# GpSimd's first loads behind a wait, and another order of the middle projection's products

## The reference, cut to what matters

```python
h  = concat(meta_tokens, x)                    # 272 rows
xn = rms_norm(h, norm_mix_g)
proj = xn @ w_in                               # q, k, v of branch A | forget, cq, ckv, k_rope, k_idx, idx_w | gates
o_a = fox_attention(...)                       # branch A, 8 heads
cq_n = rms_norm(cq); c_kv = rms_norm(ckv)      # branch B: latent attention over 64 selected keys
o_b = dsa_attention(...)
h  = h + (sigmoid(ga) * (o_a @ w_branch_a) + sigmoid(gb) * (o_b @ w_branch_b)) @ w_out
h  = h + moe_ffn(rms_norm(h))                  # top 4 of 32 experts
out = rms_norm(h)[:, 16:]
```

## Time and profile before

| | |
|---|---|
| median of 3 runs | 1213.9 us |
| lowest, highest | 1212.64, 1214.19 us |
| span of the profiled execution (first to last instruction) | 1211.7 us |
| own time of that execution | not listed apart from the three runs; its span lies 0.9 to 2.5 us under them |
| mean granted TensorE clock | 0.984 of full speed |
| busy: PE, DVE, ACT, POOL | 93%, 24%, 18%, 1% |
| DMA | 433.55 MB, mean 358 GB/s |

### The profile page before, as it was taken

One profiled execution on the slowest core, in us unless ns is written; L12 is line 12 of the kernel. 1 busy time (PEld: TensorE's weight loads), 2 busy tenths in 40 slices (PEclk: granted clock), 3 DMA queues, 4 the chain that ended last, 5 costly groups with the idle time before them and its releaser, 6 DMA issues.

```text
span 1211.7 us, 14339 instructions
## 1 busy us (share of the span) xinstructions
PE 1131.7 (93%) x5508; PEld 527.8 (44%) x5508; DVE 292.5 (24%) x726; ACT 215.0 (18%) x354; POOL 14.3 (1%) x27
## 2 busy tenths in 40 slices
PE   6999999999999999999999999989899989899986
PEld 4877788664343433343434233323333333333332
DVE  2237443241121212212212121212121212121213
ACT  1436773031011000100111011001100110011001
POOL 3010000000000000000000000000000000000000
PEclk8999999999999999999999999999999999999999
DMA  9823225849999999999999999999999999999995
GB/s 280 249 70 105 91 84 197 334 163 412 419 415 420 416 419 416 419 416 419 416 419 416 419 416 419 416 419 417 418 417 418 418 418 418 417 418 417 418 418 215
DMA packets 93306, 433.55 MB, mean 358 GB/s; under 512 B 7726, under 2 KB 24272, under 8 KB 60480
## 3 DMA queue, kind: packets, MB, share of 16 engines
q1 hardware_dynamic: 92048, 429.99, 88.2%
q0 software_dynamic: 960, 2.30, 0.8%
q10 hardware_dynamic: 272, 0.93, 0.3%
HBM read 432.13 MB, written 1.05 MB: 358 GB/s over the span
## 4 chain that ended last, share of the span: by engine, by line
PE 46%; SPq 43%; DMA 4%; DVE 4%; issue 3%; ACT 0%; DVEq 0%
SPq L438 20%; SPq L442 17%; PE psum L1535 14%; PE psum L1565 9%; SPq L449 5%; PE psum L1376 4%; PE psum L1178 2%; PE psum L1356 2%; PE psum L1394 2%; DMA arena<-in_w_gate_up 2%; PE psum L1576 2%; DMA ring<-in_w_in 2%; PE psum L1425 1%; PE psum L1340 1%; PE psum L1512 1%
## 5 line engine op out<-in xcount | busy, mean ns | idle before, releaser
L1535 PE MATMUL psum<-arena 128*64 128x512 f32 x1024 | 232.7, 598 | 12.6 <-DMA arena<-in_w_gate_up 12.6
L1535 PE MATMUL psum<-ring,arena 128*64 128x512 f32 x1024 | 232.6, 598 | 11.6 <-DMA ring<-in_w_gate_up 11.6
L1054 DVE TENSOR_TENSOR arena<-psum,biasT 128x512 f32<-128x512 f32 x64 | 44.0, 688 | 439.9 <-PE psum L1512 439.9
L1535 PEld LDWEIGHTS psum<-arena 128*64 128x64 f32 x1024 | 68.4, 137 | 162.9 <-issue 123.8
L1535 PEld LDWEIGHTS psum<-ring,arena 128*64 128x64 f32 x1024 | 68.4, 136 | 162.2 <-issue 125.1
L1565 PE MATMUL psum<-ring,arena 128*64 128x512 f32 x512 | 119.5, 623 | 17.3 <-DVE arena L1065 17.3
L1565 PE MATMUL psum<-arena 128*64 128x512 f32 x512 | 115.0, 608 | 17.3 <-DVE arena L1065 17.3
L937 DVE TENSOR_TENSOR h<-h,psum 128x1024 f32<-128x1024 f32 x32 | 39.1, 1222 | 256.6 <-PE psum L1576 256.6
L679 ACT ACTIVATE arena<-psum 128x1024 f32<-128x1024 f32 x32 | 32.8, 1025 | 351.4 <-PE psum L1535 351.4
L1565 PEld LDWEIGHTS psum<-ring,arena 128*64 128x64 f32 x512 | 39.3, 143 | 91.9 <-issue 90.4
L1565 PEld LDWEIGHTS psum<-arena 128*64 128x64 f32 x512 | 38.7, 140 | 88.0 <-issue 87.8
(11 more groups left out here) (222 smaller groups left out, 786.3 us busy)
## 6 DMA issues: line engine op xcount, KB each, us to landing
arena<-in_w_gate_up SPq DMA_DIRECT2D x128, 1024.0 KB, 22.4
ring<-in_w_gate_up SPq DMA_DIRECT2D x128, 1024.0 KB, 21.9
arena<-in_w_down SPq DMA_DIRECT2D x48, 1024.0 KB, 22.4
ring<-in_w_down SPq DMA_DIRECT2D x48, 1024.0 KB, 21.8
arena<-in_w_down SPq DMA_DIRECT2D x32, 512.0 KB, 15.8
ring<-in_w_down SPq DMA_DIRECT2D x32, 512.0 KB, 16.1
ring<-in_w_in SPq DMA_DIRECT2D x14, 1024.0 KB, 8.6
ring<-in_w_out SPq DMA_DIRECT2D x4, 1024.0 KB, 5.0
```

Of the source, the lines that this page charges most:

```text
L1054: return v.tensor_tensor(dst.rearrange("p (m j) -> p m j", m=8), src, bias[:, m:m + 8, bass.ds(pair + e, 1)].broadcast_to([P, 8, CAP]), AL ...
L1535: ins = mm(bank[2 + 2 * e + n][h * CAP:(h + 1) * CAP, :], xg[:, c, e * CAP:(e + 1) * CAP], eslot(base + k)[:, h * D + n * 512:h * D + (n + ...
```

## The change

GpSimd issues the two norm vectors as before, then waits until slot 1 has landed, and only then issues the other ten loads; `w_uv` moves behind `w_uq` and `w_qidx` among them. On TensorE the block (1, 0) comes before (0, 1): both row tiles are multiplied by weight block 0 first, then both by weight block 1, and the meta tile's transposes move from between (1, 0) and (1, 1) to ahead of (0, 1). Nothing is computed otherwise.

```diff
             vector_rows(pool, q_norm_g, LATENT, 2, s_vec2)
             vector_rows(pool, kv_norm_g, LATENT + V_KV - V_Q, 1, s_vec2)
+
+            pool.wait_ge(slot_loaded[1], 16)
             for dst, src in ((bfor, b_forget), (klng, kln_g), (klnb, kln_b), (brt, b_router)):
                 pool.dma_start(dst[:], src.broadcast_to([P, dst.shape[1]])).then_inc(s_late, 16)
             pool.dma_start(kst[:, P:KCOLS], consts[:, P:KCOLS]).then_inc(s_kst, 16)
             pool.dma_start(wuk.rearrange("p (k r) -> p k r", k=4),
                            w_uk[0].rearrange("(k a) n r -> (a n) k r", a=2)).then_inc(s_mixw, 16)
+            pool.dma_start(wq[:, :, 0:768], w_uq[0].rearrange("(c p) n -> p c n", p=P)).then_inc(s_mixw, 16)
+            pool.dma_start(wq[:, :, 768:1024], w_qidx[0].rearrange("(c p) n -> p c n", p=P)).then_inc(s_mixw, 16)
             pool.dma_start(wuv.rearrange("p (h v) -> p h v", h=HEADS),
                            w_uv[0].rearrange("h r v -> r h v")).then_inc(s_mixw, 16)
-            pool.dma_start(wq[:, :, 0:768], w_uq[0].rearrange("(c p) n -> p c n", p=P)).then_inc(s_mixw, 16)
-            pool.dma_start(wq[:, :, 768:1024], w_qidx[0].rearrange("(c p) n -> p c n", p=P)).then_inc(s_mixw, 16)
...
             input_rows(0)
             mid_block(0, 0)
             input_rows(1)
-            mid_block(0, 1)
             mid_block(1, 0)
             input_rows(2)
+            mid_block(0, 1)
             mid_block(1, 1)
```

## The result

The changed kernel takes **1203.6 us** (median of 4 runs, 1203.17 to 1203.83) against 1214.05 for the kernel before, taken beside it (4 runs): a ratio of 0.9913, 95% interval 0.9899 to 0.9927. The forecast was 1205.0 us. The profiled execution's span is 1201.4 us instead of 1211.7.

A forecast was written before the change was run, and what follows sets the result against it. The start was taken as bound by transfers until 24.2 us, then by matmuls. Strips 10.4 us earlier less 1.7 for the clock gave 8.7, 1203.0 for the span, 1205.2 for the median, stated as 1205.0; range 1202.6 to 1209.0.

The forecast's parts named there:

- One for one to the end: Start to end of kernel: each us gained at the start counts fully at the end, 8.7 us in all.
- Landings: SP queue's early loads: slot 0 at 7.4 to 8.9, tile 1 at 8.9 to 9.7, slot 1 at 11.9 to 14.8.
- the early end: SP queue's early loads: q1 alone at 0.348 MB/us lands slot 0 at 7.4, tile 1 at 8.9, slot 1 at 11.9.
- the full-clock timeline's 26.2: TensorE's start: without half-clock stretches the strips start at 26.2 in place of 36.62, 10.4 us earlier.
- one half-clock stretch, 1.7 us: TensorE's start: one 3.4 us stretch at 1.2 GHz, costing 1.7 us of the 10.4; this case had 40%.
- the hole of today whose fall came at 10.2: TensorE, kernel before: wait for slot 0 from 8.5 to 13.2; clock at half 10.2 to 17.0, reason for charging 1.7 us.
- the full-clock case: TensorE's start: no half-clock stretch, 10.4 us gained, 1203.5 us; a quarter of all chance.
- The wait's price: Before slot 1 lands: GpSimd's loads on q0 take 9.4 us of all 16 engines, which the wait removes.
- The second rival: Early loads: q0 costs only its bytes, slot 0 at 11.6, gain 6.7 us with one half-clock stretch, 1207.2 us; chance 8%.
- The first rival: Start: only the new order counts, the wait removes nothing; 4.5 us gained, 1209.4 us; chance 4%.
- The order with the wait: TensorE's start: slot 1 is wanted at 19.2 instead of 15.1 and may come 4.4 us later than the late end.
- The cover of the late loads: GpSimd's small vectors at L757: `brt` at 24.8, wanted 29.5; cover 4.7 + 4.2 = 8.9 us; slower has chance 2%.

The follow-up runs named there:

- The wait alone: The changed kernel with the old order of the products, (0, 1) before (1, 0), GpSimd's wait kept: 1203.64 us, ratio 0.9916.
- wait_slot0_new: The changed kernel with GpSimd waiting for slot 0 in place of slot 1, new order of products kept: 1204.19 us, ratio 0.9916.
- wuv_as_before: The changed kernel with the load of w_uv back ahead of w_uq and w_qidx: 1203.58 us, ratio 0.9915.
- wait_slot7: The changed kernel with GpSimd waiting for slot 7 in place of slot 1: 1211.85 us, ratio 0.9984.
- wait_slot5: The changed kernel with GpSimd waiting for slot 5 in place of slot 1: 1205.27 us, ratio 0.9928.
- order_alone: The kernel before with only the new order of the products, GpSimd's loads as before: 1208.88 us, ratio 0.9955.
- big_first: The changed kernel with constants, weights and router (2.2 MB) in front of GpSimd's wait, the four small vectors behind it: 1212.67 us, ratio 0.9983.
- small_first: The changed kernel with the four small broadcast vectors (84 KB) back in front of GpSimd's wait: 1207.81 us, ratio 0.9952.

## Why the prediction was right, and where it was off

**What bounds the start** was read rightly: two transfers until 24.2, matmuls after it. The wait alone, and the two runs that put a part of the loads back in front of it, show that GpSimd's loads were the cause.

**One for one to the end** held: 1175.2 us from the strips on against 1175.1, in a spread of 3 us over the other profiles.

**Landings.** Slot 1 was put at 13.3 between 11.9 and 14.8; GpSimd's release at 13.86 agrees, and the four further profiles that show it have 13.77 to 14.59. The bounds for the other two failed. Tile 1 was put at 8.9 to 9.7 and came at 10.5. Slot 0 was put at 7.4 to 8.9, before tile 0's features. In the changed kernel's two profiles it was there for them, but in the other six profiles with a wait in front of all ten loads and no products of zeros TensorE waited for it, until 9.42 to 9.96. The step that failed is the early end: it lets a load land when the queue has moved its own sum of bytes. The queue had moved 2.44 MB when slot 0 (1.60) released GpSimd at 9.97 in `wait_slot0_new`, and 3.85 when slot 1 (3.19) did in the changed kernel. The prediction used such a lag, 0.87 MB, for slot 3 only. What the lag is made of was not tried.

Against that, tile 0's features were ready at 8.94 instead of 9.48, which I hadn't foreseen. 0.35 us of it is VectorE's scaling of tile 0, which took 0.75 us instead of 1.10. It took 1.05 to 1.23 in the four profiles in which GpSimd was issuing weight loads at that moment, and 0.75 in the other ten. The early features and tile 1's rows, 0.5 us late for TensorE, cancel, and so the full-clock timeline's 26.2 stood at 26.16. That is luck in part: in the three other profiles with a wait, the new order and full clock (`wuv_as_before`, `wait_slot7`, `wait_slot0_new`), where slot 0 came later, the strips started at 26.74 to 27.06.

**The clock is the term that was mis-sized.** I charged one half-clock stretch, 1.7 us, "because the hole of today whose fall came at 10.2 had begun like the first of these". The changed kernel had none in either profile. It isn't that none can come: of the eight profiles with the wait on a slot, all ten loads behind it and no products of zeros, two showed one over block (0, 0). The block then took 5.25 - 3.56 = 1.7 us longer, as I had it, but the strips moved by only some 1.0, because TensorE otherwise waits 0.4 to 0.7 us for tile 1's rows behind it. So the chance was too high and the price too: the full-clock case, 1203.5, had a quarter, and 1203.6 was measured. The changed kernel's two holes, 1.1 us and 2.6 us of which 1.1 are transposes, left the granted clock at 1.00. The length of the hole alone doesn't decide it: block (0, 0) ran at half clock after 1.31 us of waiting in `wait_slot5` and at full clock after 2.42 us in `order_alone`. What the Trainium skill says of transposes (TensorE: Matmul & The Clock Gate, "Part 4: PE-mode transpose") would have made two stretches the likelier end; for holes this short no run here shows two.

**The wait's price.** The 9.4 us of q0's engine time are 2.7 for the small vectors and 6.7 for the large loads, each measured apart. Taken off today's landing they gave slot 1 well (14.8 at the latest), slot 0 and tile 1 by 0.5 to 1.1 us too early. The second rival, bytes alone, is refuted by the result's slot 0 (there by 9.04, not at 11.6) and by the small vectors, which cost 4.2 us for 84 KB. The first rival, only the order, is refuted by the wait alone. Its price of 4.5 us for the order was about right (5.4 by the medians, though the profile accounts for 2.7 of them in the strips).

**The order with the wait.** I wrote that together with the wait it gives slot 1 slack. It does, but the slack isn't needed: slot 1 came before tile 1's transposes had ended. I hadn't worked out the old order with the wait, and it would have shown that (0, 1) covers tile 1's features, 1 us that the new order leaves as a hole. Where slot 1 does come late, at 20 in `big_first`, the new order's cover is real.

**The cover of the late loads** was right in place: the 4.2 us of slack behind L757 held in the run with slot 5 (3.3 us used), and ran out in the one with slot 7 (6.1 us lost of 10.8). Ahead of L757 there was more than the 4.7 us that I counted, since `brt` landed 6.0 us after its issue in the changed kernel, not 9.8.

## What to carry to other kernels

Before a kernel's first matmuls, look at which queue holds the DMA engines, in engine time and not in bytes, and hold back the loads whose first user comes late. Count how late that user is: here a wait for slot 1 or slot 0 was free, and one for slot 7 gave nearly all of the gain back. Work out both orders of the work again once the loads are in place, because an order that filled a hole can open another. A half-clock stretch that one execution shows is a chance and not a fixed price, so look at several profiles before you count it.

## What was unexpected of the hardware

- The same four broadcast loads (0.09 MB) held the 16 engines for 2.7 us in 6 to 11 us of `small_first` and for 0.4 us in 17 to 20.4 us of the changed kernel. Early they ran beside rows of x and 984-byte rows, late beside 1 KB rows alone. Which of this makes the difference was not tried.
- The landing of the first loads varies between executions in which the loads are the same: slot 0 released block (0, 0) at 13.20 in the kernel before and at 10.95 in `order_alone`, whose loads and whose work until then are the same.
- With the wait in place a load of SP's queue counts as landed only when the queue has moved 0.6 to 0.9 MB more than the sum up to and with it: slot 1 (3.19 MB) at 3.85 MB in the changed kernel and 4.06 in the wait alone, slot 0 (1.60 MB) at 2.44 MB in `wait_slot0_new` and 2.49 in the wait alone.
- VectorE's scaling of tile 0 took 1.05 to 1.23 us in the four profiles in which GpSimd was issuing weight loads at that moment, and 0.75 us in the ten others.
